# Bias-table matmuls placed first on TensorE, and layer 0's mixer in another order of work

## The reference, cut to what matters

```python
for i in range(DEPTH):                        # DEPTH = 2
    z = x @ w_in[i]                           # 1024 -> 3328 columns
    q, k, v, u, g_attn, g_ssm = jnp.split(z, splits, axis=-1)
    a_out = sliding_window_attention(q, k, v, attn_sinks[i], rel_bias)   # adds bias[head, distance]
    s_out = s5_mixer(u, lambda, log_dt, b, c, d, w_glu, b_glu)           # state-space scan, gelu, GLU
    merged = (sigmoid(g_attn) * (a_out @ w_branch_attn[i])
              + sigmoid(g_ssm) * (s_out @ w_branch_ssm[i]))
    x = layer_norm(ALPHA * x + merged @ w_out[i], ln1_g[i], ln1_b[i])
    ffn = swiglu(x, ...) if i % 2 == 0 else moe_swiglu(x, ...)
    x = layer_norm(ALPHA * x + ffn + sigmoid(x @ ple_w_gate[i]) * (p[i] @ ple_w_proj[i]), ...)
```

## Time and profile before

| what | value |
|---|---|
| timed runs | median 1614.43 us, 1614.34 to 1617.41 |
| span of the profiled execution | 1611.1 us |
| PE busy | 1568.9 us, 97% of the span |
| weight loads of PE | 1332.2 us, 83% |
| DVE busy | 1356.8 us, 84% |
| ACT busy | 975.2 us, 61% |
| POOL busy | 160.5 us, 10% |
| moved by DMA | 456.52 MB, mean 283 GB/s |

### The profile page before, as it was taken

One profiled execution on the slowest core, in us unless ns is written; L12 is line 12 of the kernel. 1 busy time (PEld: TensorE's weight loads), 2 busy tenths in 40 slices (PEclk: granted clock), 3 DMA queues, 4 the chain that ended last, 5 costly groups with the idle time before them and its releaser, 6 DMA issues.

```text
span 1611.1 us, 23897 instructions
## 1 busy us (share of the span) xinstructions
PE 1568.9 (97%) x8952; PEld 1332.2 (83%) x8952; DVE 1356.8 (84%) x1316; ACT 975.2 (61%) x887; POOL 160.5 (10%) x151
## 2 busy tenths in 40 slices
PE   7999999999999999999999999999999999999996
PEld 5889789999899978888888888888888888888884
DVE  8976866655688788999998999998999998999998
ACT  3324444434655437776777777677777777767763
POOL 5000139950300000000000000000000000000000
PEclk9999999999999999999999999999999999999998
DMA  7434855554343557999999999999999999999993
GB/s 254 157 106 137 291 193 185 190 193 137 123 139 133 209 216 294 365 364 364 367 364 334 351 370 366 356 366 342 344 367 362 363 372 333 353 371 364 350 366 121
DMA packets 168710, 456.52 MB, mean 283 GB/s; under 512 B 7926, under 2 KB 60183, under 8 KB 168136
## 3 DMA queue, kind: packets, MB, share of 16 engines
q1 hardware_dynamic: 167880, 450.91, 77.2%
q0 software_dynamic: 768, 4.75, 0.8%
HBM read 453.01 MB, written 2.62 MB: 283 GB/s over the span
## 4 chain that ended last, share of the span: by engine, by line
PE 85%; DVE 9%; issue 3%; DMA 2%; ACT 1%; DVEq 0%; SPq 0%; ACTq 0%
PE psum L700 20%; PE psum L701 19%; PE psum L702 19%; PE psum L707 5%; PE psum L708 5%; PE psum L709 5%; PE psum L796 5%; DVE wl L457 2%; PE psum L1154 1%; DMA ring<-in_w_out 1%; PE psum L821 1%; PE psum L769 1%; DVE hid L2144 1%; DMA ring<-in_w_in 1%; DVE small L1750 1%
## 5 line engine op out<-in xcount | busy, mean ns | idle before, releaser
L457 DVE TENSOR_TENSOR wl<-ring,wh 128x2048 fp32r<-128x2048 f32 x269 | 609.6, 2289 | 66.6 <-ACT wh L451 63.0
L451 ACT ACTIVATE wh<-ring 128x2048 fp32r<-128x2048 f32 x307 | 581.4, 1918 | 124.7 <-PE psum L702 76.8
L701 PE MATMUL psum<-wl,xgh 128*128 128x512 f32 x896 | 349.0, 390 | 0.0
L700 PE MATMUL psum<-wh,xgh 128*128 128x512 f32 x704 | 282.0, 401 | 1.0 <-DVE xgl L2128 0.5
L702 PE MATMUL psum<-wh,xgl 128*128 128x512 f32 x704 | 274.9, 390 | 0.0
L701 PEld LDWEIGHTS psum<-wl,xgh 128*128 128x128 f32 x896 | 168.5, 188 | 32.3
L700 PE MATMUL psum<-wh,hidh 128*128 128x512 f32 x440 | 172.7, 393 | 3.7 <-DVE wl L457 2.9
L701 PE MATMUL psum<-wl,hidh 128*128 128x512 f32 x448 | 174.4, 389 | 0.0
L702 PE MATMUL psum<-wh,hidl 128*128 128x512 f32 x440 | 171.4, 389 | 0.0
L457 DVE TENSOR_TENSOR wl<-ring,wh_spare 128x2048 fp32r<-128x2048 f32 x72 | 164.7, 2287 | 3.0 <-ACT wh_spare L451 3.0
L700 PEld LDWEIGHTS psum<-wh,xgh 128*128 128x128 f32 x704 | 132.2, 188 | 33.8 <-DVE wl L457 5.7
(11 more groups left out here) (410 smaller groups left out, 2720.4 us busy)
## 6 DMA issues: line engine op xcount, KB each, us to landing
ring<-in_moe_gu SPq DMA_DIRECT2D x224, 1024.0 KB, 7.0
ring<-in_moe_dn SPq DMA_DIRECT2D x112, 1024.0 KB, 7.1
ring<-in_w_in SPq DMA_DIRECT2D x26, 1024.0 KB, 5.2
ring<-in_w_gu SPq DMA_DIRECT2D x22, 1024.0 KB, 5.0
ring<-in_w_dn SPq DMA_DIRECT2D x11, 1024.0 KB, 4.8
ring<-in_w_out SPq DMA_DIRECT2D x8, 1024.0 KB, 6.4
ring<-in_w_pg SPq DMA_DIRECT2D x8, 1024.0 KB, 4.9
ring<-in_w_ba SPq DMA_DIRECT2D x4, 1024.0 KB, 5.1
```

Of the source, the lines that this page charges most:

```text
L451: eng.activation(parts(u)[0], ring[:, ring_slot(u), :], ACT.Copy).then_inc(hi_ready, 1)
L457: eng.tensor_tensor(lo, ring[:, ring_slot(u), :], hi.bitcast(F32), ALU.subtract).then_inc(lo_ready, 1)
L700: pe.matmul(dst, ah, bh, start=first, stop=False, skip_group_check=True)
L701: pe.matmul(dst, ah, bl, start=False, stop=False, skip_group_check=True)
```

## The change

The two table loads go to the head of SP's list, ahead of the parameter loads, the input and the first unit. PE multiplies all eight bias rows before anything else, and ACT copies them before its two sine instructions. In layer 0, PE takes the kv unit directly behind the q units and turns the maps after it; ACT's map copies move behind the copies of keys and values. Two g steps now stand between `turn_local` and `transpose_probs(0)`, and both output halves stand together before one g step; `transpose_probs(1)`, `attend(1)` and `scores(2)` follow each other directly. Layer 1 keeps its order.

```diff
@@ block.sync
+            sp.dma_start(relb_sb[0:BUCKETS + 1], relb).then_inc(table_dma, 16)
+            sp.dma_start(hot_sb[0:BUCKETS + 1], hot_in).then_inc(table_dma, 16)
             for row, src in ((LDT, ldt_in), (LIM, lim_in), (LRE, lre_in)):
                 sp.dma_start(small[:, row, :], src).then_inc(angle_dma, 16)
             sp.dma_start(xT[:], xT_in.rearrange("(k p) n -> p k n", p=P)).then_inc(xT_dma, 16)
...
-                    if u == 1:
-                        sp.dma_start(relb_sb[0:BUCKETS + 1], relb).then_inc(table_dma, 16)
-                        sp.dma_start(hot_sb[0:BUCKETS + 1], hot_in).then_inc(table_dma, 16)
@@ block.tensor
+            bias_rows(0), bias_rows(1)
             pe.wait_ge(xT_dma, 16)
...
-                project("u")
+                project("u"), project("u"), project("q")
                 if l == 0:
-                    bias_rows(0)
-                project("u")
-                if l == 0:
-                    bias_rows(1)
-                project("q")
-                if l == 0:
-                    project("q")
-                    turn_maps(0)
-                    project("kv")
-                    local_products(0), input_states(0), turn_values(), scores(0)
+                    project("q"), project("kv")
+                    turn_maps(0), local_products(0), input_states(0), turn_values(), scores(0)
                     project("g")
-                    input_states(1)
+                    input_states(1), turn_local(0)
+                    project("g"), project("g")
+                    transpose_probs(0)
+                    project("g")
+                    attend(0), scores(1)
+                    project("g")
+                    output_states(0), output_states(1)
+                    project("g")
+                    transpose_probs(1), attend(1), scores(2)
+                    project("g")
@@ block.scalar
-            act.wait_ge(exp_in, 1)
-            act.activation(sm(SN), sm(TH), ACT.Sin).then_inc(exp_out, 1)
-            act.activation(sm(SH), sm(TH), ACT.Sin, scale=0.5).then_inc(exp_out, 1)
...
+            copy_rows(0), copy_rows(1)
+            act.wait_ge(exp_in, 1)
+            act.activation(sm(SN), sm(TH), ACT.Sin).then_inc(exp_out, 1)
+            act.activation(sm(SH), sm(TH), ACT.Sin, scale=0.5).then_inc(exp_out, 1)
...
-                    if l == 0:
-                        copy_rows(g)
...
-                if l == 0:
-                    copy_maps(0)
...
                 if l == 0:
-                    copy_local(0, 0)
+                    copy_maps(0), copy_local(0, 0)
...
+                if l == 0:
+                    gates(), copy_local(0, 1), exp_probs(0), gates(), gates(), copy_probs(0), gates(), copy_attended(0), gates()
+                    exp_probs(1), gelu_tanh(0), early_hi(12), gelu_tanh(1), gelu_hi(0), gates(), gelu_hi(1)
+                    copy_probs(1), copy_attended(1), exp_probs(2), gates(), early_hi(14)
```

More of the change, by code:

```diff
@@ L901, in _ @@
                 else:
                     input_states(0)
-                    project("q")
-                    project("kv")
+                    project("q"), project("kv")
                     input_states(1), turn_values(), scores(0)
                     project("g")
[L907 to L918, removed]
+                    turn_local(1)
+                    project("g")
+                    transpose_probs(0)
+                    project("g")
+                    attend(0), scores(1)
+                    project("g")
+                    output_states(0)
+                    project("g")
+                    output_states(1), transpose_probs(1)
@@ L921, in _ @@
+                    project("g")
+                    attend(1), scores(2)
+                    project("g")
                 u, g = state["u"], state["g"]
@@ L1363, in gelu_hi @@
                     act.activation(gsh[:, 2 * b:2 * b + 2, :], ga[:, 2 * b:2 * b + 2, :], ACT.Copy, scale=0.5).then_inc(ga_hi, 1)
[L1365 to L1369, removed]
-                if l == 0:
[L1371 to L1374, removed]
+                if l == 0:
+                    gates(), copy_local(0, 1), exp_probs(0), gates(), gates(), copy_probs(0), gates(), copy_attended(0), gates()
+                    exp_probs(1), gelu_tanh(0), early_hi(12), gelu_tanh(1), gelu_hi(0), gates(), gelu_hi(1)
+                    copy_probs(1), copy_attended(1), exp_probs(2), gates(), early_hi(14)
+                else:
+                    early_hi(7), exp_probs(0), gates(), early_hi(8)
+                    copy_local(1, 1), gates(), early_hi(9), copy_probs(0), gates(), early_hi(10), copy_attended(0)
+                    exp_probs(1), gates(), early_hi(11), gelu_tanh(0), gates(), copy_probs(1), early_hi(12), gelu_hi(0)
+                    gelu_tanh(1), gates(), copy_attended(1), early_hi(13), gelu_hi(1), exp_probs(2), gates(), early_hi(14)
                 for m in range(4):
```

## The result

The changed kernel took 1619.2 us (median of 13 runs, 1615.5 to 1622.2), the kernel before 1615.8 us beside it (13 runs). The ratio is 1.0022, with a 95% interval of 1.0014 to 1.0031: **slower by 3.4 us**, where the prediction had 3.4 us faster and a range that ended at 1614.3 us. The profiled execution of the changed kernel was its fastest (1615.5 us, span 1613.7 us). The mean granted clock of its runs goes from 0.996 in this one to 0.990, and the slower runs have the lower clock: the six from 1620.1 to 1622.2 us lie at 0.990 to 0.992, the others at 0.994 to 0.996.

A forecast was written before the change was run, and what follows sets the result against it. PE, busy 97% of the span, was taken as the bound, with one large hole at the start. -5.54 - 1.54 + 0.9 + 2.7 - 1.2 + 1.3 = -3.4 us gave 1611.0, stated as 1611.2 us, range 1609.4 to 1614.3 us.

The forecast's parts named there:

- At full clock the rows would then end at 9.1 us: Bias rows at the start: begun at 3.6 us, they end ahead of the first unit at 11.35 us.
- The term -5.54 us: Bias rows: two turns of 2.77 us each leave PE's chain if finished before the first unit lands.
- -1.54 us for a warm first projection: First projection: bias rows take over the 1.2 GHz start, so it runs at 2.4 GHz, saving 1.54 us.
- Rival 1: Clock lost: first projection slow after the gap, or clock falls in map-copy holes; price 1.5 us, 1612.7 us; chance 0.22.
- The two output halves together cost PE nothing: Output halves in a row: no cost to PE; DVE gets the first later and the second earlier.
- First unit at 12.4 us (+0.9): Start of loads: two table issues ahead delay the first unit by 0.9 us; bounds nothing and 2.0 us.
- +2.7 us for maps behind keys and values: After kv: `local_products` waits for ACT's copies, starting 6.25 us after kv instead of 3.54; bounds +2.0 and +4.0 us.
- -1.2 us for the wait at line 871: Before `transpose_probs(0)`: PE arrives one projection later, so its 1.2 us wait for DVE's softmax weights goes.
- +1.3 us for ACT's copy in front of `attend(1)`: `attend(1)` waits for ACT's copy of transposed weights, no longer under a projection: +1.3 us, bounds 0.9 and 2.5.
- The sum: All terms together, -3.4 us: span 1607.7 us, timed 1611.0 us, rounded to 1611.2 us.
- Range: Whole kernel's time: 1609.4 to 1614.3 us, leaving out the outer part of rival 2, Rival 3 and half of rival 4.
- Rival 3: Tables land late at the start, delaying bias rows; landing at 13 us makes it 4 us slower, 1618.7 us; chance 0.06.

The follow-up runs named there:

- e9: Changed kernel with zero-filled 128-row tables, small parameter loads ahead of them, and unit 13's load released by unit 10, not 9: 1611.7 us, 0.9980.
- e3: Kernel before with only the two output halves together in layer 0, one projection earlier for the second: 1619.8 us, 1.0026.
- e7: e3 with the load of unit 12 released by unit 9, not 8, so no weights load beside the output halves: 1616.0 us, 0.9997.
- e8: Kernel before with tables first, six heads' bias rows ahead of the first unit, one g step moved ahead of transpose_probs(0), ACT's list matched: 1614.2 us, 0.9987.
- e1: Kernel before with only the table loads, all bias matmuls and ACT's copies of them moved to the front: 1615.4 us, 0.9999.
- e5: Changed kernel with bias matmuls on all 128 rows, the tables filled with zeros by POOL before their loads: 1615.3 us, 0.9995.
- e4: Changed kernel with the first output half one projection earlier, so a projection stands between the halves again: 1615.7 us, 0.9994.
- e10: e8 with ACT's split of unit 14 moved behind the four GLU tanh steps: 1611.6 us, 0.9976.
- e11: e10 with all bias rows first at 128 rows, small parameter loads ahead of the tables, and keys and values ahead of the maps: 1611.1 us, 0.9974.
- e6: Kernel before with sixteen more 33-row bias matmuls (32 passes) amid projections; one execution for its profile, the added work took 17.45 us.

## Why the prediction was wrong, step by step

- **"At full clock the rows would then end at 9.1 us", and with the slow level 7.1 us for all of them:** wrong, 10.60 us. The step took the price of the slow level from another kind of matmul (one projection, +1.54 us) and let it end there. With 33 rows in use it doesn't end. The term -5.54 us (bias rows leave the path) still holds, but where the forecast had PE wait from 10.7 to 12.4 us for the first unit, it multiplied until 14.05 us: 1.65 us of loss.
- **-1.54 us for a warm first projection:** it didn't come. Five in a row take 34.79 us warm (e9) and took 36.24 us: 1.45 us lost. The forecast's own figure for five warm ones, 35.1 us, was 0.3 us too long, since projections with nothing between them lose less. Rival 1 had this loss, but by the gap ahead of the projection; there was no gap.
- **"The two output halves together cost PE nothing":** wrong, 4.65 us in the profiled execution, 4.3 us in e3's runs. The sum put it at nothing, without a row behind it. It is the larger miss, and I had no rival for it. What the runs showed in its place is a gap of 3.1 us, tied to an instruction block that comes late beside a weight load (e3, e7), and in two executions matmuls at half speed in and behind it. The order before had a projection behind each half.
- **First unit at 12.4 us (+0.9):** near. In e8, with the change's own order at the head of the loads, PE's first projection waits until 12.00 us, so +0.5 us; in the changed kernel the bias rows covered it.
- **+2.7 us for maps behind keys and values:** right, 6.25 us from the end of kv in the changed kernel, 6.26 us in e9; alone +2.1 us (1.3 to 4.2).
- **-1.2 us for the wait at line 871:** right, it is gone in the changed kernel; without the extra projection it grows to 3.5 us (e1).
- **+1.3 us for ACT's copy in front of `attend(1)`:** right, 1.30 us.
- **The sum:** -3.4 us forecast, +3.4 us measured, -3.8 us (e9) with the two causes removed. Between them lie e5, with only the rows mended, and e4, with only the halves apart. The profiled span is 2.6 us longer and w_glu 3.9 us later: 1.3 us came back behind w_glu. There the falls of the clock differ from one execution to the next: that of the changed kernel had none until 1604 us, that of the kernel before had two of 3.4 us, at 198.9 (near the 198.5 us of the earlier trace rows) and 420.7 us. What each was worth isn't shown.
- **Range:** its upper end came from mishaps of the kinds priced, ACT, DVE and late tables. Two things outside that list, the rows in use and the load of instructions, cost 1.65 + 1.45 = 3.1 us and 4.65 us, each as much as or more than the 3.1 us from forecast to bound. Rival 3 did say "slower", by up to 4 us, but for tables that land late; they were there at 3.4 us.

## What to carry to other kernels

Work moved into a wait at the start pays in full only if it ends inside that wait. Count matmuls that use 33 rows at the slow level throughout (0.66 us a pass here): six heads' rows still fitted (e8, e10), eight did not. With all 128 rows, the rest filled with zeros, the clock rises meanwhile and the work behind starts warm. Don't put several hundred very short matmuls in a row while a large load is in flight; leave a long step between, or hold the load back. And a lead of PE arrives at the end only past the next engine that sets the time (here DVE at line 871), so try the lead alone first.

## What the runs showed of the hardware that was not expected

- The granted clock fell to 0.50 at 37.1 us while PE was busy without a break on matmuls of 33 rows, and a cold PE took 844 ns a pass (482 ns when warm) through 10.6 us of them. With the other 95 rows zero it rose at 8.4 us, and in e9 and e11 at 8.0 and 10.8 us, while the bias rows ran. The Trainium skill ("TensorE: Matmul & The Clock Gate", Part 1) speaks of matmul work as such; by that the clock would have risen in the bias rows and stayed in e6. The runs decide against it for these shapes.
- PE can run out of instructions, as the timing of the instruction blocks says: 3.1, 3.2 and 3.0 us in three kernels, shown as "issue", and 0.5 and 0.3 us when the load beside them was moved. The same name also stood for a wait of 0.7 us for DVE (e4).
- In or behind such a gap the clock fell in two executions (changed kernel, e5) and not in a third (e3, the longest of the three). It also fell in a wait of 3.5 us (e1) and behind one of 2.3 us (e8). What decides it is open.
